# Reordering a fused two-block kernel: norms, delta-rule front end, router, expert ring, hand-over and attention splits

## The reference

```python
# block 1
n = rms_norm(x, norm1_w);  proj = n @ w_in                   # 1024 -> 6656 + 96 columns
c = silu(centred_dwconv(conv_in, conv_w, conv_b))            # 4608 channels, 7 taps
q, k = l2_normalize(q), l2_normalize(k)                      # 8 heads of 128, q also scaled
o = gated_delta(q, k, v, g, beta) both ways                  # needs the inverse of (I + A)
y = ssd(xs, dt, A, Bm, Cm) both ways + D * xs                # 16 heads of 64
h = x + concat(rms(o) * silu(g_gate), rms(y * silu(z))) @ w_out
n2 = rms_norm(h, norm2_w);  aff = softmax(n2 @ w_router)     # 16 experts
each expert takes its 32 best tokens: (silu(xs@w_gate) * (xs@w_up)) @ w_down * aff
x = rms_norm(h + combine, final_norm_w)
# block 2, twice
mod = silu(c) @ w_ada + b_ada
h = rms_norm(x, g_pre) * (1 + scale) + shift;  cols = h @ w_in
o_a, o_b, o_c = latent attention, window attention with sink, differential attention
x = x + gate * rms_norm((g0*(o_a@w_o) + g1*(o_b@w_o) + g2*(o_c@w_o)) @ w_out, g_post)
```

## Time and profile before

| what | value |
|---|---|
| median of 3 runs | 1417.66 us (1416.61 to 1420.83) |
| profiled execution | 1422.65 us, its span 1420.8 us |
| busy: TensorE, VectorE, ScalarE, GpSimd | 1246.5, 652.0, 406.0, 329.9 us |
| mean granted TensorE clock | 0.954 |
| ring blocks of w_ada_2, issue to landing | 8.9 us median |
| low parts (L1905) | 188.1 us busy, 68.6 us idle before them, on GpSimd's casts |
| table loads of ScalarE | 45 of 1283 ns |

### The profile page before, as it was taken

The page is one execution under the profiler, slowest core; times in us unless marked ns, Lnnn a source line. Parts: engine busy times, 40 slices in busy tenths (PEclk is TensorE's granted clock), DMA queues, the critical chain, the costliest instruction groups (busy, mean ns, idle before and its releaser), DMA issues.

```text
span 1420.8 us, 17974 instructions
## 1 busy us (share of the span) xinstructions
PE 1246.5 (88%) x7458; PEld 943.0 (66%) x7458; DVE 652.0 (46%) x1045; ACT 406.0 (29%) x975; POOL 329.9 (23%) x321
## 2 busy tenths in 40 slices
PE   6989689899889699978786999998878999899977
PEld 5878555477654442212126899898778889898867
DVE  1597748133460310001015355575786346567764
ACT  4345532133530220100004531321423451220431
POOL 0486621412300100000020212233253012223240
PEclk9999889999999699999997999999999999999998
DMA  5324223766307679999990435334332245335210
GB/s 187 128 110 157 80 89 126 259 237 226 130 1 295 231 289 420 422 421 422 421 359 1 164 118 182 119 128 169 119 107 83 75 171 179 129 114 182 91 60 30
DMA packets 90515, 256.97 MB, mean 181 GB/s; under 512 B 6605, under 2 KB 11494, under 8 KB 78018
## 3 DMA queue, kind: packets, MB, share of 16 engines
q1 hardware_dynamic: 88082, 248.61, 46.2%
q0 software_dynamic: 2032, 6.95, 1.6%
q10 hardware_dynamic: 320, 0.26, 0.1%
HBM read 253.42 MB, written 2.12 MB: 180 GB/s over the span
## 4 chain that ended last, share of the span: by engine, by line
PE 61%; DMA 13%; DVE 11%; ACT 7%; POOL 5%; issue 2%; SPq 1%; DVEq 0%; ACTq 0%; POOLq 0%
PE bank L680 57%; DMA ring<-in_w_up_dram 8%; DMA ring<-in_w_down_dram 4%; PE bank L689 4%; DVE ring_r L1905 3%; POOL late L2481 3%; POOL acc L2482 2%; DVE acc L1976 2%; ACT xT L1461 1%; DMA ring<-in_w_ada_dram 1%; ACT ring L1461 1%; ACT cT L1461 1%; ACT L1461 1%; ACT oa L1461 1%; ACT qkT L1461 0%
## 5 line engine op out<-in xcount | busy, mean ns | idle before, releaser
L2584 POOL CAST w_hi_r<-ring 128x1024 fp32r<-128x1024 f32 x136 | 152.3, 1148 | 691.3 <-DMA ring<-in_w_in_dram 273.1
L680 PE MATMUL bank<-ring_r,xT_hi 128*128 128x256 f32 (+1 forms) x864 | 247.9, 287 | 0.0
L1905 DVE TENSOR_TENSOR ring_r<-ring,w_hi_r 128x1024 fp32r<-128x1024 f32 x136 | 188.1, 1414 | 68.6 <-POOL w_hi_r L2584 68.6
L680 PE MATMUL bank<-w_hi_r,xT_hi 128*128 128x256 f32 x704 | 209.0, 297 | 6.5 <-DVE xT_r L1910 4.4
L680 PE MATMUL bank<-w_hi_r,xT_r 128*128 128x256 f32 x704 | 202.9, 288 | 0.0
L680 PEld LDWEIGHTS bank<-ring_r,xT_hi 128*128 128x128 f32 x864 | 170.4, 197 | 0.2
L680 PEld LDWEIGHTS bank<-w_hi_r,xT_hi 128*128 128x128 f32 x704 | 138.0, 196 | 19.6 <-issue 10.3
L680 PEld LDWEIGHTS bank<-w_hi_r,xT_r 128*128 128x128 f32 x704 | 137.3, 195 | 0.0
L680 PE MATMUL bank<-ring,xsT 128*32 128x512 f32 x496 | 111.6, 595 | 24.9 <-DMA ring<-in_w_up_dram 12.8
L680 PE MATMUL bank<-xT,ring 128*128 128x256 f32 x576 | 127.6, 384 | 0.0
L680 PEld LDWEIGHTS bank<-xT,ring 128*128 128x128 f32 x576 | 110.9, 193 | 15.4
(11 more groups left out here) (353 smaller groups left out, 2124.9 us busy)
## 6 DMA issues: line engine op xcount, KB each, us to landing
ring<-in_w_in_dram SPq DMA_DIRECT2D x39, 2048.0 KB, 7.6
ring<-in_w_up_dram SPq DMA_DIRECT2D x32, 1024.0 KB, 16.3
ring<-in_w_down_dram SPq DMA_DIRECT2D x32, 1024.0 KB, 16.4
ring<-in_w_gate_dram SPq DMA_DIRECT2D x30, 1024.0 KB, 16.3
ring<-in_w_ada_dram SPq DMA_DIRECT2D x12, 2048.0 KB, 8.9
ring<-in_w_out_dram SPq DMA_DIRECT2D x8, 2048.0 KB, 8.1
ring<-in_w_o_mla_dram SPq DMA_DIRECT2D x2, 2048.0 KB, 12.4
ring<-in_w_o_swa_dram SPq DMA_DIRECT2D x2, 2048.0 KB, 7.7
```

The costliest lines, as they stand in the source:

```text
L680: return release(nc.tensor.matmul(o, lhsT, rhs, start=start, stop=stop))
L1905: tt(lo, raw_, hi.bitcast(F32), ALU.subtract).then_inc(lo_done.sem, lo_done.one("piece"))
L2584: nc.gpsimd.tensor_copy(hi, raw_).then_inc(hi_done.sem, hi_done.one("piece"))
```

## The change

- Norms: ScalarE takes Sqrt alone; VectorE takes a reciprocal of 128 x 512 ahead of each of its eight multiplies; the second group comes at tile 24 and not 26 on ScalarE, at 29 and not 32 on VectorE.
- kq/decay: four buffers of E and eight banks; the first gate tile ahead of it, four banks of transposes and the second tile after it.
- Inversion: the blocks go out in four DMAs and not eight; half the inverses return over ScalarE's queue.
- w_ada_2: two blocks stand ahead of the rounds; rounds have 3, 3, 2, 2. Rows and columns have semaphores of their own.
- SSD: the first arguments ahead of the last round's o, copies earlier, its rms by Ln and Exp.
- Router: w_out's results are added by quarters; xres itself is transposed, half of it inside w_out; the logits are summed in four column groups of the array with the router weights loaded twice (32 columns) and brought together by a matmul with `same`; the norm is a scale inside the exponential; four passes on ScalarE make xn2 and its high part, GpSimd the low part; `sel` is built before `selw`; four of eight gather steps stand behind the first expert block.
- Ring: seven expert blocks are placed before the first is read (`opening`): the fourth over the place of the bias tiles, the fifth over `strips`. The DMA that fills `strips` waits until that block has been read.
- Combine, final norm and the first norm of block 2 run token tile by token tile; table loads are taken early (`warm`).
- Attention: in branches 1 and 2 a split stands behind `maxima(0)` and not ahead of it; in branch 2 `token_out(0)` follows the last `differ`; splits before the output projection are moved.

The core of the diff, line numbers left out:

```diff
--- before.py
+++ after.py
...
-    slot = [n % 2 if n < n1 else RING if n == n1 + 5 else (n - n1 + (2 if n < n1 + 5 else 1)) % RING if n < n2 else (n - n2) % (RING - 1) for n in range(len(plan))]
+    opening = (2, 3, 4, RING, RING + 1, 0, 1)
+
+    def slot_of(n):
+
+        if n < n1:
+            return n % 2
+        if n >= n2:
+            return (n - n2) % (RING - 1)
+        j = n - n1
+        return opening[j] if j < len(opening) else (j - len(opening) + 2) % RING
+
+    slot = [slot_of(n) for n in range(len(plan))]
+    over_strips = slot.index(RING + 1)
...
+                if n == over_strips:
+                    sp.wait_ge(mixT_pe.sem, 8)
...
+            def gate_tile(n, t, w):
+
+                if n == 0:
+                    pe.wait_ge(*((norm_act.sem, 8) if t == 0 else (lt_dve.sem, lt_dve.at("qkd", 7))))
+                elif n == 1:
+                    pe.wait_ge(e_act.sem, e_act.at("E", 6 + t))
+                else:
+                    pe.wait_ge(gate_act.sem, 2 * (n - 2) + t + 1)
+                    if n == 2 and t == 0:
+                        pe.wait_ge(lt_dve.sem, lt_dve.at("qkd", 6))
+                for k in range(DK):
+                    last = mm(bank[4 + 2 * (n % 2) + t][:], xT[:, k, t * P:(t + 1) * P], w[:, k, :], k == 0, k == DK - 1)
+                last.then_inc(gate_pe.sem, 1)
...
+            first_gate = take("w_in")
+            gate_tile(0, 0, first_gate)
             for h in range(GH):
                 kq_decay(h)
-            gate_block(0)
+            for i in range(4):
+                nat_bank(i)
+            gate_tile(0, 1, first_gate)
+            block_read()
             gate_block(1)
-            for i in range(9):
+            for i in range(4, 9):
                 nat_bank(i)
             gate_block(2)
             for i in range(9, 13):
...
+            for n in range(ADA[0][0]):
+                ada_rows(n, 0)
+                if n:
+                    ada_cols(n - 1)
+            pe.wait_ge(gate_act.sem, 8)
+            pe.wait_ge(nat_out.sem, 13)
             pe.wait_ge(lt_pool.sem, GH)
             for r in range(GH // 2):
-                ada_rows(3 * r, r)
+                n0, n1_, n2_ = ADA[r]
+                if r == 0:
+                    ada_cols(n0 - 1)
+                ada_rows(n0, r)
...
+        ADA = [(2, 3, 4), (5, 6, 7), (8, 9, None), (10, 11, None)]
...
+            def token_transposes(half):
+
+                for t in range(TT):
+                    pe.wait_ge(out_dve.sem, 2 * half + t + 1)
+                    for b in (2 * half, 2 * half + 1):
+                        for j in range(2):
+                            k = 2 * b + j
+                            last = tr(q4(bank[b], 2 * j + t), xres[:, t, k * P:(k + 1) * P])
+                        if t:
+                            last.then_inc(rt_pe.sem, rt_pe.one(f"x{b}"))
+
+            def logit_sums(half):
+
+                for j in range(4):
+                    k = 4 * half + j
+                    if half and j % 2 == 0:
+                        pe.wait_ge(*((rt_act.sem, rt_act.at("n2")) if j == 0 else (rt_dve.sem, rt_dve.at("n3"))))
+                    last = mm(bank[5][32 * j:32 * j + 32, 0:T], w_r[:, k, :], xT[:, k, :], half == 0, half == 1)
+                return last
...
+                        if k8 and half and t:
+                            token_transposes(0)
...
+            logit_sums(0)
+            token_transposes(1)
+            logit_sums(1).then_inc(rt_pe.sem, rt_pe.one("sums"))
+            pe.wait_ge(rt_dve.sem, rt_dve.at("sums"))
             for t in range(TT):
-                for k in range(DK):
-                    last = mm(bank[4][:, t * NE:(t + 1) * NE], xT[:, k, t * P:(t + 1) * P], w_r[:, k, :], k == 0, k == DK - 1)
+                last = mm(bank[4][:, t * NE:(t + 1) * NE], work[:, t * P:(t + 1) * P], same)
...
+            def gather(k0):
+
+                for k in range(k0, k0 + 4):
+                    if k >= 4:
+                        pe.wait_ge(gat_act.sem, k - 3)
+                    for t in range(TT):
+                        mm(bank[4 + k % 4][:], xn2_hi[:, t, k::DK], sel[:, t, :], t == 0, False)
+                    for t in range(TT):
+                        if k == 0:
+                            pe.wait_ge(rt_pool.sem, t + 1)
+                        last = mm(bank[4 + k % 4][:], xn2_r[:, t, k::DK], sel[:, t, :], False, t == TT - 1)
+                    last.then_inc(gat_pe.sem, 1)
...
+                            if gi == pair == o == k0 == 0:
+                                gather(4)
...
-                for i in range(i0, i0 + 4):
-                    f(nsq[i], nsq[i], ACT.Exp, scale=-0.5).then_inc(norm_act.sem, 1)
+                    f(nsq[i], bank[4 + i % 4][:], ACT.Sqrt, scale=float(n), bias=EPS * n).then_inc(norm_act.sem, 1)
...
-                if n in (18, 26):
-                    inverse_norms(n // 2 - 9)
+                if n in (18, 24):
+                    norms(0 if n == 18 else 4)
...
+            act.wait_ge(inv_out, 16)
+            for q in range(QN):
+                act.dma_start(Xc[q * SQ:(q + 1) * SQ, :, :, 1, :].rearrange("p h c n -> p (h c) n"), block_rows(inverses, 1, q)
+                              ).then_inc(inv_back, 16)
...
+            def high_part(t):
+
+                f(xn2[:, t, :], xres[:, t, :], ACT.Copy, scale=small[:, 6 + t:7 + t])
+                f(xn2_hi[:, t, :], xres[:, t, :], ACT.Copy, scale=small[:, 6 + t:7 + t]).then_inc(rt_act.sem, rt_act.one(f"hi{t}"))
+
             act.wait_ge(rt_dve.sem, rt_dve.at("max"))
-            f(aff[:], aff[:], ACT.Exp).then_inc(rt_act.sem, rt_act.one("exp"))
+            for t in range(TT):
+                last = f(aff[:, t, :], aff[:, t, :], ACT.Exp, scale=small[:, 6 + t:7 + t], accum_out=stat[:, 2 + t:3 + t])
+            last.then_inc(rt_act.sem, rt_act.one("exp"))
+            high_part(0)
+            high_part(1)
...
+            combine_squares(0)
+            ln_squares(0, 0)
+            combine_squares(1)
             ln_copies(0, 0)
+            ln_squares(0, 1)
+            warm(ACT.Silu)
...
+                inverse(nsq[i])
...
-                if n in (24, 32):
-                    for i in range(n // 2 - 12, n // 2 - 8):
+                if n in (24, 29):
+                    for i in range(0 if n == 24 else 4, 4 if n == 24 else 8):
...
+            combine(0)
             split_lo(0)
-            dve.wait_ge(cmb_act.sem, 1)
-            inverse(small[:, 2:4])
+            combine(1)
+            combine(2)
             dve.wait_ge(load_moe, 16 * N_MOE)
-            dve.wait_ge(cmb_dve.sem, cmb_dve.at("h1"))
-            for t in range(TT):
-                stt(out=xres[:, t, :], in0=xres[:, t, :], scalar=small[:, 2 + t:3 + t], in1=f_norm[:], op0=ALU.mult,
-                    op1=ALU.mult).then_inc(cmb_dve.sem, cmb_dve.one(f"done{t}"))
+            final_norm(0)
+            combine(3)
...
-                        split_lo(read + 1)
+                        split_lo(read - 1)
...
+                        if b and it == 0:
+                            split_lo(read + 1)
...
+                        if it == (UNITS if b == 2 else UNITS - 1):
                             token_out(0)
...
-                        if i == 2:
-                            split_lo(read + (3 if b == 2 else 2))
+                        if i == (1 if b == 2 else 2):
+                            split_lo(read + 2)
...
+                    if i == 1:
+                        split_lo(read + 1)
...
-            for d in range(2):
-                for q in range(QN):
-                    pool.dma_start(block_rows(blocks, d, q),
-                                   LT[q * SQ:(q + 1) * SQ].rearrange("p h (c d) n -> p (h c) d n", c=TT)[:, :, d, q * SQ:(q + 1) * SQ]
-                                   ).then_inc(blocks_out, 16)
-            pool.wait_ge(blocks_out, 16 * 2 * QN)
+            for q in range(QN):
+                both = bass.AP(tensor=blocks.tensor, offset=q * 32 * SQ * SQ, ap=[[SQ, SQ], [SQ * SQ, 2 * GH * TT], [1, SQ]])
+                pool.dma_start(both, LT[q * SQ:(q + 1) * SQ].rearrange("p h i n -> p (h i) n")[:, :, q * SQ:(q + 1) * SQ]
+                               ).then_inc(blocks_out, 16)
+            pool.wait_ge(blocks_out, 16 * QN)
...
+            for q in range(QN):
+                pool.dma_start(Yc[q * SQ:(q + 1) * SQ, :, :, 0, :].rearrange("p h c n -> p (h c) n"), block_rows(inverses, 0, q)
+                               ).then_inc(inv_in, 16)
...
+            pool.wait_ge(*block_free(over_strips))
```

More of the change, by code:

```diff
@@ L280, in hybrid_kernel @@
             work4 = ring[RING - 1][:]
-            E = [four(work4, 512 * i) for i in range(2)]
+            E = [four(work4, 512 * i) for i in range(4)]
+            KQ, DECAY = (0, 1, 4, 5), (2, 3, 6, 7)
             prod, Uin, Uraw = work4[:, 0:2048], work4[:, 2048:3072], work4[:, 3072:4096]
@@ L329, in hybrid_kernel @@
             strips = sb("strips", HS + HD, BIAS_W, where=st)
```

(28 more changed lines are left out.)

332 lines of the change are left out of this document (176 added, 156 removed).

## The result

The changed kernel takes 1403.47 us in the median of four runs (1401.75 to 1406.89), the kernel before 1419.24 beside it (1416.61 to 1422.47, four runs): a ratio of 0.9891, 95% interval 0.9861 to 0.9921. It is faster by 15.8 us, 1.1%; forecast was 30. The direction is right, but the gain is about half of what was forecast. The time lies 5.5 us outside my own range (1376 to 1398) and inside the wider one that took in rivals (a) and (b) (1366 to 1405); rival (b), which gave 1402 (moved splits only shift their wait), came nearer than the forecast.

What follows compares the result with a forecast made beforehand. No one engine bounds the kernel; TensorE gaps, VectorE's convolution queue and expert DMA turn edits into time. Front +10, SSD -1.5, experts -8.5, combine -10, attention -20: -30 from 1417.66 gives 1388 us, range 1376 to 1398.

Steps and rivals of the forecast that it cites:

- rival (a): Convolution norms: a 512-element reciprocal runs at an ordinary pace, 0.7 to 1 us; total -55, 1363 us; chance 0.12.
- rival (b): Attention: moved splits only shift their wait because GpSimd's casts are late; attention -6, total -16, 1402 us; chance 0.22.
- I take three quarters: -20: Attention branches, both layers: about 26 us of TensorE gaps would go, three quarters of it counted, -20 (-10 to -26).
- the ninth after the other half of the gather at about 509. From there 40 blocks: Expert stretch: 40 blocks of 5.03 us from 509, plus strips load and slot waits; end near 717.5, -8.5 us.
- rival (c): Experts: the seventh place costs, late strips load delaying bias tiles and blocks; -2 for -8.5, 1394 us; chance 0.08.
- I take -2.5: Passage from convolution to first round: -7 on TensorE's chain, most eaten by the third ada block's wait; -2.5 (0 to -7).
- SSD: Stage after the rounds: first arguments before the last round's o and earlier copies gain -1.5 us (0 to -3).
- Reciprocal: Convolution norms on VectorE: a 128x512 reciprocal takes 3.7 us (3.2 to 4.2), eight take 29.6.
- rival (d): Convolution norms: the reciprocal costs over 7.6 us, making the kernel slower; 1425 us at 8.5; chance 0.06.
- 17 us later at the end of the convolution: Convolution end: 29.6 us of reciprocals less 7.8 absorbed, 3.5 from Exp leaving ScalarE and 1 in small gaps.
- The +2 for the clock: Front: longer TensorE idle in the conv tail keeps the granted clock low a little longer, +2 us (0 to +4).
- Rounds: Rounds 2 and 3 each lose one ada block, 3.2 us apiece, -6.4 us in all.

Runs made afterwards that it cites:

- split_read: Changed kernel with split_lo(read) for split_lo(read - 1) ahead of maxima(0) in branches 1 and 2: 1379.74 us, ratio 0.9724.
- tail_old: Changed kernel with token_out(0) of branch 2 ahead of the last differ, and its last splits and those beside the y transposes as before: 1420.17 us, ratio 1.0001.
- six_places: Changed kernel with six places for expert blocks as before and the strips loaded at once: 1401.99 us, ratio 0.9877.
- strips_first: Changed kernel with seven places, but the block over the strips read first and not fifth: 1402.99 us, ratio 0.9888.
- gather_whole: Changed kernel with all eight gather steps ahead of the first expert block: 1402.54 us, ratio 0.9884.
- ssd_old: Changed kernel with first SSD arguments behind the last round, both first exponentials and the first state copy placed as before: 1400.69 us, ratio 0.9901.
- norms_exp: Changed kernel with the norms by Ln and Exp on ScalarE again and no reciprocals on VectorE: 1385.15 us, ratio 0.9758.

## Where the prediction failed and where it held

By the marks, the forecast had 10.8 us too much gain. 9.4 of it is the attention, 3.1 SSD and w_out, 2.7 the experts, 0.6 the router, 0.4 the hand-over; the front took 5.4 off.

- **Attention: the failed step, and the largest: "I take three quarters: -20".** It measured -10.6. I took split_lo(read + 1) for one split of two pieces (3.16), to be moved behind the maxima. But the new call ahead, split_lo(read - 1), stops two blocks, four pieces, short of the old one. So the two earlier pieces moved too, which the earlier trace rows does not show since they stand before its row (882.97). Four pieces behind the maxima make TensorE wait 4.89 for 3.33. split_read takes 23.7 us off with this index alone. That was rival (b) in effect, but not by its cause: GpSimd's casts were not late, they were done at 873.97 and 880.88, before the split began at 881.20:

```profile
871.93 2.04 POOL L2755 CAST w_hi_r<-ring 128x1024 fp32r<-128x1024 f32 x2 [3.62 <-PE bank L702]
878.85 2.03 POOL L2755 CAST w_hi_r<-ring 128x1024 fp32r<-128x1024 f32 x2 [4.88 <-PE bank L702]
```

  The other edits gave 17 where I had counted about 10. Their waits make up some 11 of it (3.2 at the differ and 3 at the y transposes, less what stands behind, in both layers); the rest I put down to the clock behind each gap (the eight y transposes behind the 4.12 take 1.97 us in tail_old and 1.09 in the changed kernel), but it was not added up.
- **Experts: the failed step is "the ninth after the other half of the gather at about 509. From there 40 blocks".** I let the ring refill without a stop, with 1 to 2 us for "a slot that waits for its read". Places four and five are read and not refilled, so the eleventh block waits for the sixth, and the DMA stood idle for 4.0 us between 515 and 530 (shares 0.64 and 0.55 in two slices of 5 us). Of the 13.1 us that the router gained, 7.9 were given back and not 5.2. This is rival (c) in kind: the seventh place costs 2 to 3 us. six_places, strips_first and gather_whole each bring the combine that much nearer to the start of w_out (311.4 to 312.5 us for 315.0).
- **"I take -2.5" for the passage: two sizes were off, and they nearly cancel.** The table has -0.9, which is within the spread of such a profile. The edits gain 15 (I had 7 on TensorE's chain and 5 beside it on the inversion's); the blocks ahead cost 14, not "most of the 7". I counted one wait for one block; there were two (7.01, 2.10) and their rows and columns before P5, while the kernel before had P5 beside its wait.
- **SSD** -1.5 forecast, +0.8: the early arguments left one long gap (7.26), and the granted clock was 0.50 behind it. ssd_old does not tell the two orders apart.
- **Reciprocal: right in kind, mis-sized by 10%.** 3.345 us each against 3.7; rival (a) with an ordinary pace and rival (d), over 7.6 us, are refuted by the row. An element costs six times an ordinary one (6.2 ns for 1.04). The Trainium skill ("VectorE: DVE Perf Modes", "First, the fixed hardware budget") states a repeat count of 8. Taken as eight ordinary elements, an estimate, that would be 4.3 us each; the measurement decides, and is lower.
- **The step that followed, "17 us later at the end of the convolution", is near what the reciprocals cost alone (16.7 to 19), but partly by luck.** I had them absorb the gap of 7.82, and norms_exp shows that gap at 1.07 without them. The table shows +10.7, because I gave the new places of the norm groups (24, 29) nothing and they seem worth about 6. The +2 for the clock has no mark of its own.
- **Rounds** -6.4 forecast, -5.1 measured.
- **Router** -13.7 forecast, -13.1: the sum is right, its steps by 1 to 2 us less so. To the logits it is -12.9 for -11.6 (they are ready at 481), from there to the end of the best search +4.0 for +3.2, and from there to the first expert block -4.3 for -6.2.
- **Hand-over** -10 forecast, -9.6 measured; it rests on the traces alone, its edits were not undone in a run.

## What to carry to other kernels

When a call that works off a queue "up to here" is moved, count what it will find at its new place, not what the trace shows it doing at the old one: one index was worth 24 us. An early start in front of a stretch bound by DMA is worth only what it brings the refills forward; ask when each of the first transfers that wait for a read can be issued. A filler put ahead of a chain to use idle time can cost the whole chain its own DMA wait, as the two blocks did here (14 us).

## What the runs showed of the hardware

- VectorE's reciprocal of 128x512 float32 took 3.345 us, a multiply (tensor_tensor) of that form 0.69: 6.2 ns an element by the slope from 128x8 (0.201 us), against 1.04 by the slope of tensor_tensor from 128x8 (0.164).
- A gap of TensorE of 4.89 us cost more than its length: the granted clock behind it was 0.50 from 883.6 to 886.3 and matmuls of 128x256 took 0.41 us, then 0.28 at 1.00. Four gaps of 4.89 and 4.49 us, 18.8 together, were worth 25.7 us in the trace.
- The front varies between executions of the same code, the later stages hardly: the last conv tile ended between 189.5 and 195.8 us in nine profiles of kernels that share it, while the stretch from the first projection of block 2 to the end stayed within 650.2 to 651.0 in seven. Marks are therefore compared within a profile, from one to the next.
